# An odd count of expert items: pairs in the loop and a single item behind it

## The chip, the cores and the metric

The kernel runs on one core of a Trainium2 chip. The metric is the device time of one execution in microseconds (us). Before the change three executions took 1818.12, 1817.78 and 1817.76 us, a median of 1817.78.

## The reference

The reference is one layer of a decoder: an HGRN2 recurrence and a gated short convolution side by side, an output projection with a residual, then a mixture of experts, and a last RMS norm. The change touches the routed experts alone:

```python
T = 1024 tokens (16 meta tokens ahead of them are dropped at the end), D_MODEL = 1024
N_EXPERTS, TOP_K, EXPERT_FF = 64, 8, 256

scores = sigmoid(xt @ w_router)
_, top_idx = top_k(scores + router_bias, TOP_K)
gates = scores[top_idx] / sum(scores[top_idx]) * 2.5
for each expert e, for each token t that chose it:
    routed[t] += gate[t, e] * (silu(x[t] @ w_gate_e[e]) * (x[t] @ w_up_e[e])) @ w_down_e[e]
```

There are 1024 x 8 = 8192 assignments, 128 to an expert in the mean.

## The kernel before

**Items.** The routed work is cut into items. One item is one expert with up to CAP = 160 of its tokens; an expert with more than 160 gets further items. So there are 64 + X items, where X counts the further ones. The table of items has room for ITEMS = 118; unused entries are padding: they name an expert, but their rows lie behind the real ones (rows 1024 and up) and their gates are zero.

An item's tokens are 128 main rows (gathered to `XG`) and up to 32 rest rows. The rest rows of two items (a pair, with q = 0 and q = 1) are gathered together (to `XR`, 64 rows). Per item the kernel turns X by TensorE transposes (L1510, and L1518 for the pair's rest), computes gate and up in float32 (L1530, 64 matmuls), sigmoid and products (ScalarE L1614, VectorE L1670 to L1676), splits the down matrix into a high and a low part (`WH` on ScalarE L1601, `WL` on VectorE L1665), and computes down for the rest rows in float32 (L1541, 16 matmuls) and for the main rows from the parts (L1552 to L1554, 12 matmuls). ScalarE evicts the results with the gate as scale (`YF` L1620, `YE` twice in L1624), and POOL adds them to the accumulator in HBM by two indirect DMAs with an addition, the rest rows from `YF` (L1449) and the main rows from `YE` (L1453).

**How many.** `phase_out_route` writes the count of pairs less one to `K.pairs` (L1291 to L1293): 31 plus the number of the entries of `twos` (0, 2, 4, ... from the iota in L923) that are below X. Each engine reads it as `last`.

**Turns.** Every engine runs `turn_(i, q, ahead)` with n = 2i + q. In a turn, TensorE first computes gate and up of item n + 1 (`ahead` of 1 or more), turns the rows of item n + 2 (`ahead` of 2; for q = 0 the next pair's rest rows too), and then does down of item n (`down_rest`, then `down` twice). The loop runs full turns for i from 0 to last - 1. Behind it, written out, stand the turns of the last pair: `turn_(last, 0, 1)` and `turn_(last, 1, 0)`.

**Queues around it.** SP loads the weights in the loop: in each turn gate and up of item n + 3 (L1408), once TensorE is done with gate and up that lie in that place, and down of item n + 2 (L1409), once VectorE and `down_rest` are done with item n. At its end it waits for the last gate and up (L1412). POOL in each turn copies the gates of item n + 1, waits until TensorE has turned, and gathers item n + 4 (L1422) and for q = 0 the rest rows of pair i + 2 (L1430). Then `add_rows` (L1438) waits until both scatters of item n - 1 have landed (`s_ad`, L1441), copies the indices (L1444), waits for `YF` and issues L1449, waits for `YE` and issues L1453. At the end it waits until all of them have landed (L1499); after that block comes `phase_final`, whose first load of the accumulator is L1718.

Of the kernel before, what the change touches and what calls it, by code (L numbers as in the profile page):

```python
# [775 lines left out]
def phase_out_route(nc, ins, K, xn2_d, acc_d, tbl_d):  # L776
# [4 lines left out]
    with ExitStack() as ctx:  # L781
# [130 lines left out]
        @block.gpsimd  # L912
        def _(pool):
            pool.memset(junk, 0.0).then_inc(s_z, 1)
            pool.iota(fill[:, :, 0], [[1, CAP]], base=T, channel_multiplier=0, allow_small_or_imprecise_dtypes=True).then_inc(s_fi, 1)
            pool.memset(fill[:, :, 1:2], 0.0).then_inc(s_fi, 1)
            pool.memset(before[:, :], 1.0).then_inc(s_k0, 1)
            pool.memset(pairsel[:, :], 1.0).then_inc(s_k0, 1)
            pool.iota(lowi[:, :], [[0, 1]], base=0, channel_multiplier=1, allow_small_or_imprecise_dtypes=True).then_inc(s_k0, 1)
            pool.iota(rowc[:, :], [[0, 1]], base=0, channel_multiplier=CHUNKS, allow_small_or_imprecise_dtypes=True).then_inc(s_k0, 1)  # L920
            pool.iota(e0[:, :], [[CHUNKS * CAP, E_N]], base=1, channel_multiplier=0, allow_small_or_imprecise_dtypes=True).then_inc(s_k, 1)
            pool.iota(pidx[:, :], [[0, 1]], base=-E_N, channel_multiplier=1, allow_small_or_imprecise_dtypes=True).then_inc(s_k, 1)
            pool.iota(twos, [[2, 32]], base=0, channel_multiplier=0, allow_small_or_imprecise_dtypes=True).then_inc(s_k, 1)  # L923
            pool.iota(pay[:, :, :, 0], [[P, TT], [0, TOPK]], base=0, channel_multiplier=1,
                      allow_small_or_imprecise_dtypes=True).then_inc(s_k, 1)
            pool.wait_ge(s_k0, 4)

            pool.affine_select(out=before[:, :], in_=before[:, :], compare_op=ALU.is_gt, fill=0.0,
                               base=0, pattern=[[1, P]], channel_multiplier=-1).then_inc(s_k, 1)
            pool.affine_select(out=pairsel[:, :], in_=pairsel[:, :], compare_op=ALU.is_ge, fill=0.0,  # L930
                               base=0, pattern=[[-2, PAIRS]], channel_multiplier=1).then_inc(s_k0, 1)
            pool.wait_ge(s_k0, 5)
            pool.affine_select(out=pairsel[:, :], in_=pairsel[:, :], compare_op=ALU.is_ge, fill=0.0,
                               base=1, pattern=[[2, PAIRS]], channel_multiplier=-1).then_inc(s_k, 1)

            pool.wait_ge(s_fo, 16 * -(-TABLE_ROWS // P))
            for j in range(TT):
                pool.wait_ge(s_pay, j + 1)
                for k in range(TOPK):
                    pool.indirect_dma_start(tbl_d, bass.IndirectOffsetOnAxis(ap=si[:, j * TOPK + k:j * TOPK + k + 1], axis=0),  # L940
                                            pay[:, j, k, :], None).then_inc(s_sca, 16)
            pool.wait_ge(s_row, 1)
            pool.wait_ge(s_sca, 16 * TT * TOPK)
            pool.indirect_dma_start(tbl.rearrange("i c w -> i (c w)"), None, tbl_rows,
                                    bass.IndirectOffsetOnAxis(ap=rowi[:, :], axis=0)).then_inc(s_ti, 16)
            pool.wait_ge(s_ag, 16 * len(SLOT_TILES))
            pool.memset(K.slot[2][2 * CAP1:, :], 0.0).then_inc(s_xr, 1)
            pool.wait_ge(s_ix, 1)
            pool.indirect_dma_start(K.slot[0], None, xn2_d, bass.IndirectOffsetOnAxis(ap=K.idx[0][:, 0:1], axis=0)) \
                .then_inc(K.s_g[0], 16)  # L950
            pool.wait_ge(s_xr, 1)
            pool.indirect_dma_start(K.slot[2][0:2 * CAP1, :], None, xn2_d, bass.IndirectOffsetOnAxis(ap=K.rest[:, 0:1], axis=0)) \
                .then_inc(K.s_gr, 16)
            pool.indirect_dma_start(K.slot[1], None, xn2_d, bass.IndirectOffsetOnAxis(ap=K.idx[0][:, 1:2], axis=0)) \
                .then_inc(K.s_g[1], 16)
            pool.wait_ge(s_ti, 16)
# [373 lines left out]
def phase_experts(nc, ins, K, xn2_d, acc_d):  # L1330
# [3 lines left out]
    with ExitStack() as ctx:  # L1334
# [46 lines left out]
        @block.sync  # L1381
        def _(sp):
            def load(n, q, matrices):

                e = sp.value_load(K.expert[0:1, bass.ds(n, 1)], min_val=0, max_val=E_N - 1)
                for k in matrices:
                    src = weights[k]
                    if k == 2 and not isinstance(n, int):
                        sp.wait_ge(s_dlo, n - 1)
                        sp.sem_inc(turn["sp"], 1)  # L1390
                        sp.wait_ge(s_yr, n - 1)
                        sp.sem_inc(turn["sp"], 1)
                    elif k == 0:
                        sp.wait_ge(s_gu, n * 2 - 2)
                        sp.sem_inc(turn["sp"], 1)
                    sp.dma_start(WR[q][k][:, :].rearrange("p (o t f) -> p o t f", o=1, t=src.shape[2]), src[:, bass.ds(e, 1), :, :]) \
                        .then_inc(s_raw[q][k], 16)

            for q in two:
                for k in two:  # L1400
                    sp.sem_inc(s_raw[q][k], 16)
            sp.sem_inc(s_raw[0][2], 16)
            load(1, 1, (2,))
            load(2, 0, (0, 1))
            last = pairs(sp)
            with sp.Fori(0, last) as i:
                for q in two:
                    load(i * 2 + (q + 3), 1 - q, (0, 1))  # L1408
                    load(i * 2 + (q + 2), q, (2,))  # L1409

            for k in two:
                sp.wait_ge(s_raw[0][k], last * 16 + 32)  # L1412
                sp.sem_inc(turn["sp"], 1)

        @block.gpsimd
        def _(pool):
# [72 lines left out]
                for q in two:  # L1489
                    turn_(i, q, 2)  # L1490
            for q in two:
                turn_(last, q, 1 - q)

            for q in two:
                pool.wait_ge(s_g[q], last * 16 + 32)
                pool.sem_inc(turn["pool"], 1)
            pool.wait_ge(s_gr, last * 16 + 32)
            pool.sem_inc(turn["pool"], 1)
            pool.wait_ge(s_ad, last * 64 + 64)  # L1499
            pool.sem_inc(turn["pool"], 1)  # L1500

        @block.tensor
        def _(pe):
# [83 lines left out]
            with pe.Fori(0, last) as i:  # L1587
                for q in two:
                    turn_(i, q, 2)
            for q in two:  # L1590
                turn_(last, q, 1 - q)

        @block.scalar
        def _(act):
# [31 lines left out]
            def turn_(i, q, ahead):  # L1626
                n = i * 2 + q
                high_down(q, n, i + 1)
                if ahead >= 1:
                    sigmoid(0, n + 1)  # L1630
                if ahead >= 2:
                    keep(0, q, n + 2)
                    keep(1, q, n + 2)
                if ahead >= 1:
                    sigmoid(1, n + 1)
                if ahead >= 2 and q == 0:
                    keep_rest(0, i + 1)
                    keep_rest(1, i + 1)
                evict_rest(q, n)
                for g in two:  # L1640
                    evict(q, n, g)
# [10 lines left out]
            with act.Fori(0, last) as i:  # L1652
                for q in two:
                    turn_(i, q, 2)
            for q in two:
                turn_(last, q, 1 - q)

        @block.vector
        def _(dve):
            step = Chain(dve, s_hc)  # L1660
            tt = nc.vector.tensor_tensor

            def low_down(q, n):
                dve.wait_ge(s_dhi, n + 1)
                tt(WL[q][:, :], WR[q][2][:, :], WH[q][:, :].bitcast(F32), ALU.subtract).then_inc(s_dlo, 1)  # L1665

            def hidden(f, q, n):

                dve.wait_ge(s_ss, n * 2 + f + 1)
                step(tt(SS[:, f, :], SS[:, f, :], gu[f][:, 0, :], ALU.mult))  # L1670
                if f == 0:
                    dve.wait_ge(s_y, n * 2 + 1)
                step(tt(HF[q][:, f, :], SS[:, f, :], gu[f][:, 1, :], ALU.mult))
                dve.sem_inc(s_gk, 1)
                step(nc.vector.tensor_copy(HH[q][:, f, :], HF[q][:, f, 0:P]))
                tt(HL[q][:, f, :], HF[q][:, f, 0:P], HH[q][:, f, :].bitcast(F32), ALU.subtract).then_inc(s_he, 1)  # L1676

            def turn_(i, q, ahead):
                n, o = i * 2 + q, 1 - q
                low_down(q, n)  # L1680
                if ahead >= 1:
                    hidden(0, o, n + 1)
                    hidden(1, o, n + 1)

            hidden(0, 0, 0)
            hidden(1, 0, 0)
            last = pairs(dve)
            with dve.Fori(0, last) as i:
                step.enter(i, 12)
                for q in two:  # L1690
                    turn_(i, q, 2)
            step.leave(last)
            for q in two:
                turn_(last, q, 1 - q)


def phase_final(nc, ins, K, acc_d, out):
# [89 lines left out]
```

## Time and profile before

| what | before |
|---|---|
| median of three executions | 1817.78 us |
| the profiled execution, its time | 1817.95 us |
| its span, first to last instruction | 1816.2 us |
| mean granted TensorE clock | 0.965 of full speed |
| the stage of the experts | about 841 to 1791 us of the span |
| the final norm behind it | 1791 to 1816 us |

The profile is of one execution. The span leaves out what lies around the first and the last instruction, so it is 1.75 us shorter than that execution's time. The engines are PE (TensorE's matmuls), PEld (its weight loads, which overlap them), DVE (VectorE), ACT (ScalarE), POOL (GpSimd) and SPq (the DMA issues of SyncE). A row of the timeline gives start and duration in us, engine, line, operation, and in brackets how long the engine sat idle ahead of it and what ended that.

### The profile page before, as it was taken

Reading aid. Unit: us, or ns where it says so; the run is one execution under the profiler, and the core shown is the slowest. Engines: PE = TensorE matmul, PEld = TensorE weight load, DVE = VectorE, ACT = ScalarE, POOL = GpSimd, SP = SyncE. Lnnn points to the kernel's source line nnn. Section 1 sums busy time; section 2 is a strip of 40 time slices with the busy share of each in tenths; the row PEclk is TensorE's granted clock in tenths of the full one; section 3 lists DMA queues with packets and bytes.
Section 4 is the critical chain, followed back from the end, with each engine's and each line's share of the span. In section 5 each row is a group of like instructions: output and inputs, shape, how many; then the busy total and the mean of one; then the engine's idle time right before and its main releaser. Section 6 shows DMA issues by size and latency. Waiting matters only on the chain. (4 is left out here: it accounts for less than half of the span.)

```text
span 1816.2 us, 29882 instructions
## 1 busy us (share of the span) xinstructions
PE 1686.2 (93%) x10076; PEld 1336.2 (74%) x10076; DVE 737.5 (41%) x1532; ACT 632.8 (35%) x1004; POOL 644.0 (35%) x790
## 2 busy tenths in 40 slices
PE   4989899999998899997999999999999999999981
PEld 3767655655554356675999999999999999999970
DVE  5010266666665676541333333333333333333332
ACT  7111233333333332111434433444344334443433
POOL 1200000025552122331544554445455444554540
PEclk9989899999999899998999999999999999999995
DMA  4011100010006101143999999999999999999986
GB/s 141 1 47 35 35 24 23 23 34 24 23 12 250 65 24 48 47 163 131 305 319 322 318 322 312 323 325 313 318 316 317 327 310 323 328 310 320 321 259 222
DMA packets 111949, 348.68 MB, mean 192 GB/s; under 512 B 14591, under 2 KB 48064, under 8 KB 94510
## 3 DMA queue, kind: packets, MB, share of 16 engines
q1 hardware_dynamic: 78094, 260.23, 39.7%
q0 software_dynamic: 33824, 88.06, 20.0%
q8 instruction: 16, 0.26, 0.1%
q14 instruction: 15, 0.12, 0.0%
HBM read 290.46 MB, written 57.79 MB: 192 GB/s over the span
## 5 line engine op out<-in xcount | busy, mean ns | idle before, releaser
L1530 PE MATMUL gu<-XS,place 128*128 128x160 f32 x4224 | 597.1, 300 | 0.7 <-ACT XS L1609 0.7
L1530 PEld LDWEIGHTS gu<-XS,place 128*128 128x128 f32 x4224 | 584.3, 190 | 6.2 <-ACT XS L1609 1.1
L1665 DVE TENSOR_TENSOR WL<-place,WH 128x2048 fp32r<-128x2048 f32 x66 | 152.1, 2305 | 339.0 <-ACT WH L1601 339.0
L469 PE MATMUL bank<-xT,wi 128*128 128x512 f32 x512 | 241.6, 613 | 0.0
L1614 ACT ACTIVATE SS<-gu 128x160 f32<-128x160 f32 x132 | 40.2, 304 | 372.3 <-PE gu L1530 372.3
L469 PEld LDWEIGHTS bank<-xT,wi 128*128 128x128 f32 x512 | 93.5, 194 | 90.4 <-issue 90.4
L1670 DVE TENSOR_TENSOR SS<-SS,gu 128x160 f32<-128x160 f32 x132 | 41.7, 316 | 261.1 <-ACT SS L1614 261.1
L357 POOL TENSOR_TENSOR place<-place 128x514 f32<-128x514 f32 (+1 forms) x8 | 12.0, 1494 | 371.5 <-ACT place L539 371.2
L1435 POOL COPY gta<-tables 128x1 f32 (+1 forms) x66 | 130.4, 1977 | 11.7 <-POOLq L781 11.7
L1624 ACT ACTIVATE YE<-ype,gta 128x512 f32<-128x512 f32 x132 | 91.0, 690 | 112.4 <-PE ype L1554 112.4
L940 POOL DMA_INDIRECT slot_table<-pay,si x64 | 63.2, 988 | 183.7 <-DVEq L1238 166.7
L1449 POOL DMA_INDIRECT acc_rows<-YF,sib x66 | 105.4, 1596 | 61.1 <-POOL sib L1444 56.6
L1601 ACT ACTIVATE WH<-place 128x2048 fp32r<-128x2048 f32 x66 | 125.5, 1902 | 0.7 <-issue 0.7
L1453 POOL DMA_INDIRECT acc_rows<-YE,sia x66 | 112.0, 1697 | 27.5 <-issue 24.5
L1552 PE MATMUL ype<-WH,hidh 128*128 128x512 f32 x264 | 111.4, 422 | 0.0
L1554 PE MATMUL ype<-WH,hidr 128*128 128x512 f32 x264 | 104.2, 395 | 0.0
L1553 PE MATMUL ype<-WL,hidh 128*128 128x512 f32 x264 | 103.8, 393 | 0.0
L1435 POOL COPY gtb<-tables 128x1 f32 (+1 forms) x66 | 92.1, 1396 | 0.0
L1422 POOL DMA_INDIRECT wi<-xn_rows,gi x66 | 67.3, 1020 | 55.1 <-POOL gi L1419 55.1
L458 PEld LDWEIGHTS sc<-wi 128*128 128x128 f32 x448 | 57.5, 192 | 34.5 <-issue 34.0
L1605 ACT COPY XS<-xp 128x512 f32<-128x512 f32 x132 | 71.0, 589 | 31.1 <-PE xp L1510 22.5
L1552 PEld LDWEIGHTS ype<-WH,hidh 128*128 128x128 f32 x264 | 49.8, 189 | 36.0 <-issue 27.6
(279 smaller groups left out, 2506.0 us busy)
## 6 DMA issues: line engine op xcount, KB each, us to landing
place<-in_w_gate_e SPq DMA_DIRECT2D x67, 1024.0 KB
place<-in_w_up_e SPq DMA_DIRECT2D x67, 1024.0 KB
place<-in_w_down_e SPq DMA_DIRECT2D x66, 1024.0 KB
wi<-in_w_in SPq DMA_DIRECT2D x16, 512.0 KB, 3.9
xn_rows<-place SPq DMA_DIRECT2D x9, 512.0 KB, 2.6
xt<-in_x SPq DMA_DIRECT2D x8, 512.0 KB, 5.7
wbuf<-in_w_in SPq DMA_DIRECT2D x8, 512.0 KB, 4.1
wo<-in_w_out SPq DMA_DIRECT2D x2, 2048.0 KB, 10.2
```

The source lines that it names most:

```text
L469: last = pe.matmul(bank[blk][:, :], wbuf[s][:, t, :], K.xT[:, t, cols], start=(t == 0), stop=(t == KT - 1))
L1435: last = pool.tensor_copy(gt[q][r][:, :], K.gate[r][:, bass.ds(n, 1)])
L1449: pool.indirect_dma_start(acc_q, bass.IndirectOffsetOnAxis(ap=si[q][1][:, :], axis=0), YF[q][:, :], None, compute_op=ALU.add).then_inc(s_a ...
L1453: pool.indirect_dma_start(acc_d, bass.IndirectOffsetOnAxis(ap=si[q][0][:, :], axis=0), YE[q][:, :], None, compute_op=ALU.add).then_inc(s_a ...
L1530: last = pe.matmul(gu[f][:, k, :], raw[:, t, f * P:f * P + P], XS[:, q, t, :], start=(t == 0), stop=(t == KT - 1))
L1552: pe.matmul(yp[g][:, :], hh, high[:, f, cols], start=(f == 0), stop=False)
L1553: pe.matmul(yp[g][:, :], hh, low[:, f, cols], start=False, stop=False)
L1554: last = pe.matmul(yp[g][:, :], hl, high[:, f, cols], start=False, stop=(f == 1))
L1601: act.activation(WH[q][:, :], WR[q][2][:, :], ACT.Copy).then_inc(s_dhi, 1)
L1605: act.copy(XS[:, q, 4 * h:4 * h + 4, 0:P], xp[h][:, :, :]).then_inc(s_xk, 1)
L1624: act.activation(YE[q][:, 512 * g:512 * g + 512], yp[g][:, :], ACT.Copy, scale=gt[q][0][:, 0:1]).then_inc(s_ya, 1)
L1665: tt(WL[q][:, :], WR[q][2][:, :], WH[q][:, :].bitcast(F32), ALU.subtract).then_inc(s_dlo, 1)
```

## The change

The iota starts from 1 in place of 0, so `K.pairs` counts 1, 3, 5, ... below X. TensorE, ScalarE and VectorE get three written-out turns behind the loop: a full one for q = 0, one that looks a single item ahead for q = 1, and one that only finishes item 2 * last + 2. POOL's three turns gather nothing more. SP loads the down matrix of the single item behind the loop (its gate and up come from the loop) and doesn't wait at its end. POOL's last wait counts two more DMAs (32) beside `last`.

```diff
@@ phase_out_route, gpsimd
-            pool.iota(twos, [[2, 32]], base=0, channel_multiplier=0, allow_small_or_imprecise_dtypes=True).then_inc(s_k, 1)
+            pool.iota(twos, [[2, 32]], base=1, channel_multiplier=0, allow_small_or_imprecise_dtypes=True).then_inc(s_k, 1)
@@ phase_experts, sync
-            for k in two:
-                sp.wait_ge(s_raw[0][k], last * 16 + 32)
-                sp.sem_inc(turn["sp"], 1)
+            load(last * 2 + 2, 0, (2,))
@@ phase_experts, gpsimd
             for q in two:
-                turn_(last, q, 1 - q)
+                turn_(last, q, 1)
+            turn_(last + 1, 0, 0)
...
-            pool.wait_ge(s_ad, last * 64 + 64)
+            pool.wait_ge(s_ad, last * 64 + 96)
@@ phase_experts, tensor, and the same in scalar and vector
-            for q in two:
-                turn_(last, q, 1 - q)
+            turn_(last, 0, 2)
+            turn_(last, 1, 1)
+            turn_(last + 1, 0, 0)
```

## Rows read from the trace of the kernel before

**Rows 1.** The page: its span and the first of its engines.
```profile
span 1816.2 us, 29882 instructions
PE 1686.2 (93%) x10076; PEld 1336.2 (74%) x10076; DVE 737.5 (41%) x1532; ACT 632.8 (35%) x1004; POOL 644.0 (35%) x790
```

**Rows 2.** Groups by line, 700 to 1816 us: busy, mean ns, idle before.
```profile
L1530 PE MATMUL gu<-XS,place 128*128 128x160 f32 x4224 | 597.1, 300 | 0.7 <-ACT XS L1609 0.7
```

**Rows 3.** DMA issues of the whole run: count, KB each, us to landing.
```profile
place<-in_w_gate_e SPq DMA_DIRECT2D x67, 1024.0 KB
...
place<-in_w_down_e SPq DMA_DIRECT2D x66, 1024.0 KB
...
wi<-xn_rows,gi POOLq DMA_INDIRECT x66, 7.6
```

**Rows 4.** Stretches: length, busy PE, PEld, DVE, ACT, POOL, clock, DMA, GB/s.
```profile
1500.00:1700.00 200.00, 200.00 (x1487) 182.47 (x1486) 64.23 (x127) 82.28 (x129) 100.68 (x130) 1.00 1.01 321
```

**Rows 5.** PE's waits, 800 to 1816 us: total us, times, longest.
```profile
PE yrest L1541 <- DVE WL L1665: 5.1, 1, 5.1
PE xp L1510 <- PEq L781: 4.6, 1, 4.6
```

**Rows 6.** Timeline, the first down_rest matmul of a turn (for 882.32 its weight load).
```profile
882.32 0.59 PEld L1541 LDWEIGHTS yrest<-place,HF 128*32 128x32 f32 x16 [0.17 <-issue]
...
1720.71 1.07 PE L1541 MATMUL yrest<-place,HF 128*32 128x256 f32 x16
...
1735.12 1.07 PE L1541 MATMUL yrest<-place,HF 128*32 128x256 f32 x16
...
1748.66 1.07 PE L1541 MATMUL yrest<-place,HF 128*32 128x256 f32 x16
...
1761.31 1.07 PE L1541 MATMUL yrest<-place,HF 128*32 128x256 f32 x16
...
1770.41 1.94 PE L1541 MATMUL yrest<-place,HF 128*32 128x256 f32 x16 [5.09 <-DVE WL L1665]
```

**Rows 7.** SP: two loads of the timeline, and one of SP's waits.
```profile
1734.54 0.34 SPq L1396 DMA_DIRECT2D place<-in_w_gate_e  x1
...
1736.48 0.39 SPq L1396 DMA_DIRECT2D place<-in_w_down_e  x1
...
SPq L1413 <- DMA place<-in_w_gate_e: 5.1, 1, 5.1
```

**Rows 8.** Timeline, the last turns: evictions, WL, POOL's scatters, first load behind.
```profile
1724.77 0.69 ACT L1624 ACTIVATE YE<-ype,gta 128x512 f32<-128x512 f32 x1 [0.67 <-PE ype L1554]
...
1726.24 1.56 POOL L1453 DMA_INDIRECT acc_rows<-YE,sia  x1 [0.84 <-ACT YE L1624]
...
1740.70 1.57 POOL L1453 DMA_INDIRECT acc_rows<-YE,sia  x1 [0.40 <-issue]
...
1741.72 2.31 DVE L1665 TENSOR_TENSOR WL<-place,WH 128x2048 fp32r<-128x2048 f32 x1 [5.65 <-ACT WH L1601]
...
1751.63 0.18 POOL L1444 COPY sia<-tables 128x1 int32 x1 [4.96 <-DMA acc_rows<-YE,sia]
...
1765.36 0.69 ACT L1624 ACTIVATE YE<-ype,gta 128x512 f32<-128x512 f32 x1 [0.67 <-PE ype L1554]
...
1767.88 2.29 DVE L1665 TENSOR_TENSOR WL<-place,WH 128x2048 fp32r<-128x2048 f32 x1 [4.74 <-ACT WH L1601]
1768.33 3.26 POOL L1453 DMA_INDIRECT acc_rows<-YE,sia  x1 [0.30 <-issue]
...
1776.22 0.19 POOL L1444 COPY sia<-tables 128x1 int32 x1 [4.63 <-DMA acc_rows<-YE,sia]
...
1776.89 0.69 ACT L1624 ACTIVATE YE<-ype,gta 128x512 f32<-128x512 f32 x1 [0.95 <-PE ype L1554]
...
1779.34 1.54 POOL L1453 DMA_INDIRECT acc_rows<-YE,sia  x1 [0.30 <-issue]
...
1791.05 0.33 SPq L1718 DMA_DIRECT2D A<-acc_rows  x1
```

More of the change, by code:

```diff
@@ L1654, in _ @@
                     turn_(i, q, 2)
-            for q in two:
-                turn_(last, q, 1 - q)
+            turn_(last, 0, 2)
+            turn_(last, 1, 1)
+            turn_(last + 1, 0, 0)
         @block.vector
@@ L1692, in _ @@
             step.leave(last)
-            for q in two:
-                turn_(last, q, 1 - q)
+            turn_(last, 0, 2)
+            turn_(last, 1, 1)
+            turn_(last + 1, 0, 0)
 def phase_final(nc, ins, K, acc_d, out):
```

## The prediction

> **What bounds the kernel now.** I read the page first, for the span and the engines [rows 1]: TensorE is busy for 93% of 1816.2 us. Then I read the groups of the routed experts' stage and its DMA issues [rows 2, 3]. There are 4224 gate and up matmuls, 64 to an item, so 66 items are computed; 67 gate matrices, as many up matrices and 66 down matrices are loaded, and 66 main gathers start inside the stage (the first two are issued ahead of it). So the queue fetches more than the items need. Next comes the question which of TensorE and DMA sets the pace, since the stretch table has both full: TensorE 200.00 of 200.00 us, DMA share 1.01, 321 GB/s, clock 1.00 [rows 4]. TensorE's list of waits settles it: in the whole stage it waited 4.6 us for its own sequencer at the start and 5.1 us for WL at the end, and never for a transfer [rows 5]. Its timeline says the same by turns. I take the first `down_rest` matmul of each item as a mark (turn n computes gate and up of item n+1 and down of item n). From 1720.71 to 1735.12 is 14.41 us, a turn with q=0, which also turns the rest rows; from there to 1748.66 is 13.54 us, a turn with q=1 [rows 6]. These two numbers alternate over the whole stage: from the mark at 882.32 to that at 1748.66 are 31 pairs of turns in 866.34 us, 27.95 a pair, which is 14.41 + 13.54. A stage paced by a memory queue would not repeat so exactly. The last two turns are shorter, 12.64 and 9.10 us, since they have less ahead to compute.
>
> **How many items there must be.** The table gives 64 + X items, where X counts experts' further chunks of 160 tokens. The reference's router on its own inputs, less the 16 meta tokens, gives the largest loads as 165, 160, 155 and 154 of 8192 assignments: X = 1. (66 items in the trace fit X = 1 or 2.) Before, the pair count is 31 + ceil(X/2) = 32, with two more turns behind the loop. After, iota base 1 makes it 31 + floor(X/2) = 31, with three turns behind the loop: 65 items, and item 65, which was all padding, is gone.
>
> **The parts, costed.**
> - *TensorE.* Before: 32 pairs of full turns, then the turn with gate and up only, then down alone. After: 31 pairs, one full q=0 turn written out, then the same two short ones. The difference is exactly one full q=1 turn: 13.54 us [rows 6], all of it on the path, as TensorE has no idle time there.
> - *Code.* The q=0 turn now runs outside the loop. No row shows that turn there, so I bound it. Above stands TensorE's 4.6 us wait for its sequencer at the stage's start [rows 5]; below stands 0, as the short turn behind the loop began without idle time (12.64 us, a q=1 turn without its transposes). A gain is excluded, since full turns in the loop already have no gap. I take 0, the nearer row, being the same loop's exit. ScalarE and VectorE have idle time in each turn. The iota's new base costs nothing: same instruction, and not near the end of anything.
> - *SP's queue.* Loads of 5 matrices fall away: gate, up and down of item 65, gate and up of item 66. Item 64's down load is issued at the same place in its turn as before, behind `down_rest` of item 62 (near 1736.5, the place of the row at 1736.48 [rows 7]), and is needed one turn later, near 1752.4; it now has no 2 MB of gate and up from 1734.54 ahead of it. SP's closing wait for item 66's gate and up goes (the gate's alone was 5.1 us [rows 7]), on a queue that then had nothing to do until 1791. Worth 0.
> - *POOL's queue.* Two gathers and a rest gather (items 66 and 67) go, with their index copies. POOL waits in each turn for the landing of the previous item's scatters, so here it matters what follows the PE work. I work it out in the clock of before.
>  PE, ScalarE and VectorE do turns up to 62 as before, so item 62's YE scatter starts at 1740.70 or up to 0.5 earlier [rows 8]. In before it landed so that POOL moved on at 1751.63, 10.9 us later, in a full DMA. With the weights gone I take 7.9 us, the time from 1768.33 to 1776.22, where DMA was nearly idle: 1748.6. Then YF of item 63 and, 0.8 us behind the eviction, YE follow (the lag: an eviction ending at 1725.46 and a scatter at 1726.24 [rows 8]). Item 63's last eviction ends at 1766.05 - 13.54 = 1752.5, so YE is issued at 1753.3, in place of 1768.33 - 13.54 = 1754.8. It thus starts ahead of WL (1767.88 - 13.54 = 1754.34). In before it started behind WL's start and took 3.26 us in place of 1.54. It ends at 1754.9 and lands 4.6 us later (1771.59 to 1776.22), at 1759.5. The last item's YE then no longer waits for POOL's chain but for its own eviction, which ends at 1776.89 + 0.69 - 13.54 = 1764.04: issue at 1764.84, against 1779.34 - 13.54 = 1765.80. Gain: **0.96 us**. Bounds: 0, if the landing stays at 10.9 us, and about 2, if the last scatter also lands sooner because YF's rows, issued 1.9 us ahead of it, are out of its way. I take 0.96, since DMA in that stretch will be like the near-idle one.
> - *The end.* From the last YE issue to the first load of the final norm is 11.71 us (1779.34 to 1791.05), and 25.2 us behind it. Unchanged.
>
> The 3.26 us row is a long scatter issue that starts inside WL. A page of the Trainium skill has a rule on this (SBUF — State Buffer, SBUF: two separate sides): VectorE and GpSimd share a port pair under an exclusive lock, and descriptors aren't written while VectorE holds it. Read strictly, item 63's YE would end only behind WL, near 1757.2, land near 1761.8, and let the last YE go at 1764.96; the sum would be 14.4 in place of 14.5. The row at 1740.70 (1.57 us, though WL ran from 1741.72) speaks against the strict reading.
>
> **Sum:** 13.54 + 0.96 = 14.5 us. The profiled execution is 1817.95 us (span 1816.2 and 1.75 around it), so 1803.45 and a span of 1801.7. The median of three runs lies 0.17 below it: **1803.3 us**.
>
> **The rivals.**
> 1. *The tail keeps its chain.* Only the turn goes and POOL's waits shift whole: 1817.78 - 13.54 = 1804.2. For it: the last three turns' order on every queue is the same. Against it: DMA load there falls. 18%.
> 2. *A stall behind the loop.* The unrolled turn waits for code on TensorE by the 4.6 us of [rows 5]: 1803.3 + 4.6 = 1807.9. Against it: no gap at the loop's exit now. 6%. The Trainium skill (Runtime: NRT & Kernel Launch, Instruction fetch mechanics) says that a taken branch breaks sequential fetch and straight code does not; by that rule nothing is added here, as in my sum.
> 3. *DMA is the pace.* Then what counts is bytes: 5 matrices of 1.05 MB, two gathers of 0.52, a rest gather of 0.26 and scatters of 0.66, together 7.2 MB, at 321 GB/s [rows 4] 22.4 us: 1795.4. For it: a DMA share of 1.01. Against it: the waits and the exact turns. 3%.
> 4. *Slower: X is even.* If the router on the chip gives the expert with 160 tokens one more, X = 2; before it is 66 items all the same, but the changed kernel then does 67, a padded one at the end. The price is one q=0 turn: 1817.78 + 14.41 = 1832.2, less up to 1 in the tail. It decides at one token. For it: 160 is on the edge, and the trace cannot tell 65 from 66 real items. Against it: it needs a near tie to fall otherwise than in the reference. 2%.
>
> **How the numbers follow.** My forecast has 70%, with 1 for what I have not named, near no change. The range is the forecast's bounds and the first rival with some spread of the runs (0.36 us before): 1801.8, from a tail gain of 2 and 0.5 for spread, to 1804.9, from no tail gain and 0.7 for spread. A measurement of this kernel can tell about 0.2%, 3.6 us, from no change. Faster by more: 0.97 (the forecast and rivals 1, 2 and 3). Slower: 0.02 (rival 4). The same: 0.01.
>
> **What would show it.** The page should have 65 WL subtractions, 4160 gate and up matmuls, 65 loads of each matrix, 64 main gathers and 32 rest gathers in the stage. The marks should run 14.41, 12.64, 9.10 at the end, the last near 1756.86. The penultimate YE issue should take about 1.55 us and not 3.26, and the last come near 1764.8 with its wait ended by ScalarE's eviction. The final norm's first load should start near 1776.5. I am wrong if there are 67 items, if a gap stands between the loop and the next turn, or if turns in the loop are not 14.41 and 13.54.

## The result and the profile after

| what | before | after |
|---|---|---|
| median, range of the executions | 1817.77 us (1817.58 to 1818.12, four) | 1803.24 us (1801.18 to 1805.14, four) |
| ratio after to before, 95% interval | | 0.9913 (0.9898 to 0.9928) |
| the profiled execution | 1817.95 us | 1801.69 us |
| its span | 1816.2 us | 1799.9 us |

The change takes 14.5 us off the medians. The forecast was 1803.3. That the two agree to 0.1 us is partly luck: the four executions after it spread over 4 us, and the two profiled ones lie 16.3 us apart. In two later sets of executions (below) both kernels ran some 5 us faster, and the changed kernel's median lay 14.2 and 13.6 us below that of before. So I read the result from the traces, stage by stage.

The page of the changed kernel, its span and engines [rows 1], a group [rows 2], and its DMA issues [rows 3]:

```profile
span 1799.9 us, 29556 instructions
PE 1671.2 (93%) x9976; PEld 1323.4 (74%) x9976; DVE 734.7 (41%) x1523; ACT 627.0 (35%) x996; POOL 636.3 (35%) x778
...
L1529 PE MATMUL gu<-XS,place 128*128 128x160 f32 x4160 | 587.4, 299 | 0.7 <-ACT XS L1609 0.7
...
L1420 POOL DMA_INDIRECT wi<-xn_rows,gi x64 | 65.0, 1015 | 53.4 <-POOL gi L1417 53.4
...
place<-in_w_gate_e SPq DMA_DIRECT2D x65, 1024.0 KB
```

4160 gate and up matmuls are 65 items; a gate matrix is loaded once for each, in place of 67 times for 66. X is 1, as worked out from the reference's router: 66 items before allow X = 1 or 2, and with X = 2 the changed kernel would compute 67.

The stretch table of the changed kernel, same columns as [rows 4], and TensorE's waits [rows 5], from 700 us on:

```profile
1500.00:1700.00 200.00, 200.00 (x1491) 182.68 (x1490) 65.24 (x127) 81.67 (x128) 101.57 (x129) 1.00 1.01 322
```

```profile
PE yrest L1540 <- DVE WL L1666: 5.1, 1, 5.1
PE xp L1509 <- PEq L781: 4.6, 1, 4.6
```

The steady part is the same, and no new wait stands among the written-out turns. Its timeline, the first `down_rest` matmul of the last turns [rows 6], and the first mark of the stage:

```profile
867.66 1.07 PE L1540 MATMUL yrest<-place,HF 128*32 128x256 f32 x16
...
1719.60 1.07 PE L1540 MATMUL yrest<-place,HF 128*32 128x256 f32 x16
...
1734.01 1.07 PE L1540 MATMUL yrest<-place,HF 128*32 128x256 f32 x16
...
1746.67 1.07 PE L1540 MATMUL yrest<-place,HF 128*32 128x256 f32 x16
...
1755.77 1.94 PE L1540 MATMUL yrest<-place,HF 128*32 128x256 f32 x16 [5.08 <-DVE WL L1666]
```

The marks of the last items are 14.41, 12.66 and 9.10 us apart: the full q=0 turn, now outside the loop, takes what it took inside. The tail on POOL, ScalarE and VectorE [rows 8]:

```profile
1739.71 1.54 POOL L1451 DMA_INDIRECT acc_rows<-YE,sia  x1 [0.30 <-issue]
...
1746.20 0.18 POOL L1442 COPY sia<-tables 128x1 int32 x1 [3.15 <-DMA acc_rows<-YE,sia]
...
1752.19 1.54 POOL L1451 DMA_INDIRECT acc_rows<-YE,sia  x1 [1.47 <-ACT YE L1624]
1753.24 2.29 DVE L1666 TENSOR_TENSOR WL<-place,WH 128x2048 fp32r<-128x2048 f32 x1 [4.74 <-ACT WH L1601]
...
1758.68 0.18 POOL L1442 COPY sia<-tables 128x1 int32 x1 [4.95 <-DMA acc_rows<-YE,sia]
...
1760.75 1.57 POOL L1447 DMA_INDIRECT acc_rows<-YF,sib  x1 [1.76 <-issue]
1761.91 0.69 ACT L1624 ACTIVATE YE<-ype,gta 128x512 f32<-128x512 f32 x1 [0.70 <-PE ype L1553]
1763.38 1.54 POOL L1451 DMA_INDIRECT acc_rows<-YE,sia  x1 [1.06 <-ACT YE L1624]
...
1774.94 0.34 SPq L1720 DMA_DIRECT2D A<-acc_rows  x1
```

The last but one YE scatter is issued ahead of WL and takes 1.54 us, where it took 3.26 behind WL's start; it lands earlier, and the last one waits for its own eviction ("ACT YE") and no longer for POOL's chain ("issue").

**Where the 16.3 us between the two traces went.** I cut each trace at three instants: the first mark of the stage (868.78 before, 867.66 after), the last mark, and the last YE issue; the final norm's first load is the fourth.

| stretch | before | after | difference |
|---|---|---|---|
| start to the first mark | 868.78 | 867.66 | 1.12 |
| first mark to last mark | 901.63 | 888.11 | 13.52 |
| last mark to last YE issue | 8.93 | 7.61 | 1.32 |
| last YE issue to the final norm's first load | 11.71 | 11.56 | 0.15 |
| behind that | 25.15 | 24.96 | 0.19 |

The first row is no work of the change, since that code is the same but for the iota's base; the first mark stands at 867.66, 864.59 and 863.61 in the three traces of the changed kernel. The number that carries the rest is **first mark to the final norm's first load: 922.27 us before, 907.28 after, 14.99 less**. I compare the experiments by it. The kernel before was traced once, so 922.27 is one execution's number; three traces of the changed kernel give 907.28, 907.14 and 907.19.

### The profile page after: what moved, and what is told of

Same layout as the page of the kernel before. It is cut to its first block and busy times, and to the rows that moved or that the text cites. A ratio compares the mean times of both kernels' runs of the same rounds, so it can differ in the third digit from the quotient of the medians.

```text
span 1799.9 us, 29556 instructions
## 1 busy us (share of the span) xinstructions
PE 1671.2 (93%) x9976; PEld 1323.4 (74%) x9976; DVE 734.7 (41%) x1523; ACT 627.0 (35%) x996; POOL 636.3 (35%) x778
## 5 line engine op out<-in xcount | busy, mean ns | idle before, releaser
L1529 PE MATMUL gu<-XS,place 128*128 128x160 f32 x4160 | 587.4, 299 | 0.7 <-ACT XS L1609 0.7
L1529 PEld LDWEIGHTS gu<-XS,place 128*128 128x128 f32 x4160 | 574.9, 190 | 6.0 <-ACT XS L1609 1.1
L357 POOL TENSOR_TENSOR place<-place 128x514 f32<-128x514 f32 (+1 forms) x8 | 11.4, 1422 | 369.9 <-ACT place L539 369.6
L1433 POOL COPY gta<-tables 128x1 f32 (+1 forms) x65 | 126.0, 1938 | 10.5 <-POOLq L781 10.5
L1451 POOL DMA_INDIRECT acc_rows<-YE,sia x65 | 116.5, 1792 | 30.0 <-issue 24.7
L1433 POOL COPY gtb<-tables 128x1 f32 (+1 forms) x65 | 83.5, 1285 | 0.0
L1540 PE MATMUL yrest<-place,HF 128*32 128x256 f32 x1040 | 70.5, 389 | 5.1 <-DVE WL L1666 5.1
```

The lines of the kernel that those rows point to most:

```text
L1433: last = pool.tensor_copy(gt[q][r][:, :], K.gate[r][:, bass.ds(n, 1)])
L1451: pool.indirect_dma_start(acc_d, bass.IndirectOffsetOnAxis(ap=si[q][0][:, :], axis=0), YE[q][:, :], None, compute_op=ALU.add).then_inc(s_a ...
L1529: last = pe.matmul(gu[f][:, k, :], raw[:, t, f * P:f * P + P], XS[:, q, t, :], start=(t == 0), stop=(t == KT - 1))
L1540: last = pe.matmul(yr[j * CAP1:(j + 1) * CAP1, :], HF[q][:, f, P:CAP], raw[:, f, j * DQ:(j + 1) * DQ], start=(f == 0), stop=(f == 1), tile ...
```

## The experiments

The experiments ran in three sets. In two of them the kernel before itself spread over 1808.37 to 1815.18 us (15 executions, median 1812.12) and 1808.28 to 1817.46 us (11, median 1812.36); in the third, of a single execution of each kernel, it took 1818.01. So their medians tell a microsecond from another poorly, and their traces tell it well. "Stage" below is first mark to the final norm's first load.

**The changed kernel again.**

> The changed kernel unchanged, to see its spread. Its four times fell in two pairs, 1801.2 and 1801.7, 1804.8 and 1805.1, where before spreads over 0.5 us. Theory A (the turn and the tail come off exactly; the spread comes from the stages ahead of the experts, where the granted clock rises at other moments): in the trace the marks from the first full turn on stay 14.41 and 13.54 apart and the tail as seen, and a time that differs does so ahead of 880 us. Theory B (the tail behind the loop is what varies, as its DMA order is new): the marks before 1700 us agree to 0.5 us and the difference stands behind them. Median 1801 to 1805 by both.

Measured: 1797.93 us (1795.05 to 1798.57, five), ratio 0.9915 (0.9902 to 0.9929), so 14.2 us less than before again. Stage 907.14 us, 0.14 from the first trace, though its first mark stands at 864.59 and not at 867.66. Theory A holds, with one correction: the clock makes its difference in the tail too (below). The gain is the same on a base that moves.

**The useless transfers put back.** The excerpt leaves out POOL's waits at its end and the bound of the item table.

```diff
+            load(last * 2 + 3, 1, (0, 1))
             load(last * 2 + 2, 0, (2,))
+            for k in two:
+                sp.wait_ge(s_raw[1][k], last * 16 + 32)
+                sp.sem_inc(turn["sp"], 1)
@@ gpsimd
-            for q in two:
-                turn_(last, q, 1)
+            turn_(last, 0, 2)
+            turn_(last, 1, 1)
...
```

> The changed kernel with useless transfers put back in the last full turn: gate and up of item 65 (2 MB) ahead of item 64's down matrix, waited for by SP at the end, and the gathers of item 66 and its rest rows. 65 items as in the change. Theory A (a part of the gain is the DMA load that falls away in the tail, so that POOL's chain of scatters no longer sets the end): slower than the changed kernel by 1.0 to 1.5 us, about 1804.2, with the last but one YE scatter issued inside WL and 3.26 us long again. Rival (the tail shifts as a whole and these transfers cost nothing): within 0.3 us of the changed kernel, its scatters where they were.

Measured: 1800.11 us (1799.04 to 1804.22, five), 0.9934 (0.9920 to 0.9947). Stage 908.72 us, 1.44 and 1.58 above the two traces of the changed kernel, and 13.55 below before: one q=1 turn, 13.54. That the two agree to 0.01 us is luck in part, as the last YE issue comes 9.11 us behind the last mark (8.93 before) and the final norm's first load 11.50 us behind that (11.71 before). Its timeline:

```profile
1747.00 0.19 POOL L1446 COPY sia<-tables 128x1 int32 x1 [7.63 <-DMA acc_rows<-YE,sia]
...
1749.56 2.29 DVE L1670 TENSOR_TENSOR WL<-place,WH 128x2048 fp32r<-128x2048 f32 x1 [4.75 <-ACT WH L1605]
...
1750.07 3.20 POOL L1455 DMA_INDIRECT acc_rows<-YE,sia  x1 [0.30 <-issue]
...
1758.08 0.18 POOL L1446 COPY sia<-tables 128x1 int32 x1 [4.82 <-DMA acc_rows<-YE,sia]
...
1759.33 1.57 POOL L1451 DMA_INDIRECT acc_rows<-YF,sib  x1 [0.94 <-POOL sib L1446]
1761.20 1.54 POOL L1455 DMA_INDIRECT acc_rows<-YE,sia  x1 [0.30 <-issue]
```

The scatter before lands late (7.63 us of waiting in place of 3.15), the next is issued inside WL and takes 3.20 us, and the last is set by POOL's chain. That is before's tail, on a kernel with 65 items. The slow link is the third YE scatter from the end: from its issue to POOL's next index copy are 11.10 us here (1735.90 to 1747.00), and 6.49 in the changed kernel (1739.71 to 1746.20). The other traces agree: 8.9 to 11.1 us in the four where the transfers run on (10.12 before), 6.4 to 6.8 us in the eight where they are gone and such a copy follows the landing. So the fallen transfers shorten the chain, and the rival, that the tail shifts whole, is out. This run puts weights and gathers back together and doesn't tell which of them delays the scatter.

How much of that reaches the end is another question. The last eviction ends 7.53 us behind the last mark here and 6.83 in the changed kernel, as the granted clock rose later (6.0 against 4.5 us behind the mark). A last YE issue 0.78 us behind its eviction, as in the changed kernel, would have come at 8.31 and not 9.11: POOL's chain costs 0.8 us here, and by the same reckoning 1.0 before (8.93 for 7.17 + 0.78). The other 0.7 is the clock's. The kernel with 64 items (below) has the useless transfers too, and its chain came through in time:

```profile
1739.31 1.54 POOL L1453 DMA_INDIRECT acc_rows<-YE,sia  x1 [0.57 <-issue]
...
1740.37 2.29 DVE L1665 TENSOR_TENSOR WL<-place,WH 128x2048 fp32r<-128x2048 f32 x1 [4.75 <-ACT WH L1601]
...
1751.09 1.54 POOL L1453 DMA_INDIRECT acc_rows<-YE,sia  x1 [2.45 <-ACT YE L1624]
```

There the slow scatter took 9.25 us, the next one was issued ahead of WL, and the last one waited for its eviction, which ended 7.41 us behind the mark. So the useless transfers cost 0.8 and 1.0 us at the end of two traces and nothing in that one.

**Only the useless transfers taken away, 66 items.** The excerpt leaves out the bounds of the pair count and POOL's last wait, which counts two more items.

```diff
-            step(ts(K.pairs[:, :], pr, float(E_N // 2 - 1), None, ALU.add))
+            step(ts(K.pairs[:, :], pr, float(E_N // 2 - 2), None, ALU.add))
@@ behind the loop of tensor, scalar and vector
             for q in two:
-                turn_(last, q, 1 - q)
+                turn_(last, q, 2)
+            for q in two:
+                turn_(last + 1, q, 1 - q)
@@ behind the loop of gpsimd
             for q in two:
-                turn_(last, q, 1 - q)
+                turn_(last, q, 1)
+            for q in two:
+                turn_(last + 1, q, 1 - q)
@@ sync
+            load(last * 2 + 3, 1, (0, 1))
+            load(last * 2 + 2, 0, (2,))
+            load(last * 2 + 3, 1, (2,))
...
```

> The kernel before with its 66 items, but the last full pair written out behind the loop, so that nothing is loaded or gathered for items 66 and 67. Theory A: 1.0 to 1.5 us faster than before, about 1816.5, from the tail alone, with all turns 14.41 and 13.54 apart and the last mark at the same place as before (1770.4 less what the start of the stage gives). Rival 1 (nothing in the tail depends on it): within 0.3 us of before. Rival 2 (written-out turns wait for code): slower than before, by up to 4.6 us at the loop's exit. Rival 3 (DMA is the pace): faster by 2 matrices and two and a half gathers, 3.4 MB or 10 us.

Measured: 1811.37 us (1807.97 to 1814.56, eleven), 0.9997 (0.9988 to 1.0007), so the times show no difference. Stage 921.67 us, only 0.60 below before, where I expected 1.0 to 1.5. Its marks still alternate and end with 13.54, 12.64, 9.11, so a loop left one pair earlier costs nothing, and rival 3, DMA as the pace (10 us), is out. POOL's part came as expected: the last index copy stands 2.90 us behind the last mark (1766.24 to 1763.34) and not 5.81 (1776.22 to 1770.41). The rest was given back at the last eviction:

```profile
1763.34 1.94 PE L1543 MATMUL yrest<-place,HF 128*32 128x256 f32 x16 [5.09 <-DVE WL L1671]
...
1770.32 0.69 ACT L1628 ACTIVATE YE<-ype,gta 128x512 f32<-128x512 f32 x1 [1.46 <-PE ype L1556]
...
1771.78 1.54 POOL L1453 DMA_INDIRECT acc_rows<-YE,sia  x1 [2.72 <-ACT YE L1628]
```

TensorE idles 5.1 us ahead of the last down, and the granted clock is at 0.50, half of 2.4 GHz, when it starts again. When it rises differs from execution to execution: 4.5 us behind the last mark in the changed kernel's trace, 5.2 before, 6.3 here. The last eviction ended 6.83, 7.17 and 7.67 us behind the mark, in the same order. Since now the eviction sets the end, the 0.5 us between here and before counts; without it the gain would be 1.0 to 1.1.

**67 items, the parity falling the other way.**

```diff
-            step(ts(K.pairs[:, :], pr, float(E_N // 2 - 1), None, ALU.add))
+            step(ts(K.pairs[:, :], pr, float(E_N // 2), None, ALU.add))
```

> The changed kernel with a pair count higher by one, so that it computes 67 items, the last two all padding: the price of the parity falling the other way. Theory A: the changed kernel plus one pair of turns, 14.41 + 13.54 = 27.95 us, about 1831.2, and 14.4 less up to 1.3 in the tail above before, so 13.0 to 13.5 slower than before. Rival (padded items cost less or more than real ones, since their gathers and scatters go to neighbouring rows): the turns of items 65 and 66 would stand out from 14.41 and 13.54.

Measured: 1823.67 us (1822.86 to 1825.98, four), 1.0065 (1.0050 to 1.0080) of before, 11.6 us above its median. Stage 935.89 us: 13.62 above before (13.0 to 13.5 expected; the clock rose 5.4 us behind the last mark, and the last eviction ended 7.23 behind it), and 28.6 above the changed kernel (27.95). The turns that compute gate and up of the padded items 65 and 66 take 14.41 and 12.66 us (marks from 1739.91 to 1754.32 and 1766.98), as the same turns do with real ones. So rival 4's price was right by the traces (the medians give less, 11.6): with an even count this change costs nearly what it gains with an odd one. It is a stand-in: no run had a router that gives X = 2.

**64 items.**

```diff
-            pool.iota(twos, [[2, 32]], base=0, channel_multiplier=0, allow_small_or_imprecise_dtypes=True).then_inc(s_k, 1)
+            pool.iota(twos, [[2, 32]], base=1, channel_multiplier=0, allow_small_or_imprecise_dtypes=True).then_inc(s_k, 1)
```

> The kernel before with the iota's base at 1 alone, so it does 64 items and leaves out the item of the fullest expert's last 5 tokens. Together with the others it gives a ladder of 64, 65, 66 and 67 items. Theory A: from the first mark of the stage to the final norm's first load 27.95 us less than before's 922.27, so 894.3, and the changed kernel's 907.1 to 907.3 lies a q=0 turn above it less the tail's 1.3 to 1.5, so 13.0 above. Rival (the last items, as padding, are cheaper): not on this ladder.

Measured: 1792.56 us in its single execution; stage 895.97 us, 1.65 above the 894.3 expected, so the changed kernel stands only 11.3 above it and not 13.0. The marks are right (the last at 1742.90, 873.68 behind the first; before's 901.63 less 27.95 is 873.68). The last YE issue comes 0.74 sooner behind its mark than before (8.19, as above). From there to the final norm's first load it takes 14.10 us, where 11.4 to 11.8 is what all the others take. The DMA engines move nothing more from 1757 on, 8 us ahead of that load, so it is no slow transfer. I have no explanation for these 2.4 us.

**Which engine is the pace.** Two kernels, the changed one with fewer bytes and the changed one with fewer matmuls, each executed once (1795.36 and 1739.07 us):

> The changed kernel with only half of each up matrix loaded in the stage (0.52 MB less of about 4.5 MB in every turn; the other half of the place keeps what an earlier item left, so the result is not the reference's). Theory A (TensorE is the pace): marks 14.41 and 13.54 apart as before, the span within its spread, only POOL's waits for landed scatters shorter. Rival (DMA is the pace): each turn 12% shorter, 1.6 us, and 100 us off the whole.

> The changed kernel without the matmuls that multiply the low part of the down matrix (L1552 of the changed kernel, 4 of 0.23 us in a turn; the result loses that part's precision). Theory A: turns of 13.49 and 12.62 us, 60 us off the whole, as long as DMA follows: the same bytes in a turn shorter by 0.92 us are 343 GB/s in place of 321. Rival (DMA is just as full as TensorE): turns stay near 14.41 and 13.54, and TensorE's list shows waits for the gate and up loads.

```profile
1300.00:1500.00 200.00, 200.00 (x1492) 182.64 (x1492) 66.83 (x131) 81.11 (x130) 102.67 (x130) 1.00 0.96 282
```

```profile
1300.00:1500.00 200.00, 200.00 (x1533) 183.87 (x1532) 71.14 (x140) 86.63 (x139) 102.69 (x141) 1.00 1.03 341
...
PE yrest L1540 <- DVE WL L1665: 5.1, 1, 5.1
```

The first row is the kernel with half of each up matrix: 282 GB/s in place of 322, and turns of 14.41 and 13.54 still (stage 907.12 us). The second is the kernel without the low product, with its only wait of TensorE from 860 us on: turns of 13.51 and 12.63, 58.6 us off the stage (848.68), and DMA simply moved 341 GB/s at a share of 1.03. So a DMA share of 1.01 didn't mean that DMA was full. TensorE is the pace, by removal and not only by its list of waits.

**The long scatter issue.**

```diff
@@ vector, the very last turn of the kernel before
-                low_down(q, n)
+                low_down(q, n, ahead == 0)
@@ vector, low_down
                 dve.wait_ge(s_dhi, n + 1)
+                if skip:
+                    dve.sem_inc(s_dlo, 1)
+                    return
```

> The kernel before without VectorE's computation of the low part in the very last turn (it signals at once; the last item's low part is that of an earlier one, so its result is not the reference's; that item is padding). Theory A (a scatter issue that starts inside this instruction is held up by it): the last but one YE scatter's issue is 1.55 us long in place of 3.26, though nothing of POOL is changed, and the last mark comes 2.3 us sooner behind its neighbour, at 6.8 in place of 9.10. Rival (the long issue comes from something else, such as descriptors waiting for room): it stays at 3.2 us.

```profile
1763.51 1.54 POOL L1453 DMA_INDIRECT acc_rows<-YE,sia  x1 [0.30 <-issue]
```

Measured: 1812.34 us in its single execution. The issue takes 1.54 us in place of 3.26, and the last mark stands 6.84 us behind its neighbour. But this run alone doesn't show the cause. POOL saw the scatter ahead land sooner than before (8.94 us behind its issue, and not 10.12), so this issue started at 1763.51, while WH was still being made:

```profile
1762.31 1.90 ACT L1601 ACTIVATE WH<-place 128x2048 fp32r<-128x2048 f32 x1
```

WL couldn't have started before 1764.21, so with WL in place the issue would have been ahead of it all the same. What ties the long issues to WL is the timing over all thirteen traces. 94 of the 1698 scatter issues of the stage take longer than 1.65 us (2.04 to 3.67). Each of them starts inside WL, 0.06 us or more behind its start, and each ends 1.42 to 1.44 us behind WL's end, wherever inside it started. All the others take 1.54 to 1.65 us; among them are the only five that started inside WL by less, at most 0.04 us. One of the 94, from the loop of the kernel with the transfers put back (ends at 1724.78 and 1726.22):

```profile
1722.49 2.29 DVE L1670 TENSOR_TENSOR WL<-place,WH 128x2048 fp32r<-128x2048 f32 x1 [4.75 <-ACT WH L1605]
...
1722.79 3.43 POOL L1455 DMA_INDIRECT acc_rows<-YE,sia  x1 [0.30 <-issue]
```

So a long issue is one that waits for WL to end. The Trainium skill (SBUF — State Buffer, SBUF: two separate sides) says that VectorE and GpSimd share a port pair under an exclusive lock, which whichever starts first keeps for its whole instruction. The timing agrees with that for a scatter that starts inside WL; that it is a port, no run shows. For a scatter that starts first the traces show no delay, be it by 1 us ([rows 8] at 1740.70) or by 0.08, as these rows of the changed kernel show:

```profile
1726.10 1.56 POOL L1451 DMA_INDIRECT acc_rows<-YE,sia  x1 [0.30 <-issue]
1726.18 2.29 DVE L1666 TENSOR_TENSOR WL<-place,WH 128x2048 fp32r<-128x2048 f32 x1 [4.75 <-ACT WH L1601]
```

That fits the page too. The strict reading in the prediction, by which such a scatter would end only behind WL, is wrong.

**A shorter tail.** The 5.1 us of idle time ahead of the last down come from order alone: WH of the last item stands on ScalarE behind the evictions, though its weights landed long before. In the last turn but one both engines have idle time:

```diff
@@ scalar, turn_
-                high_down(q, n, i + 1)
                 if ahead >= 1:
+                    high_down(q, n, i + 1)
                     sigmoid(0, n + 1)
+                if ahead == 1:
+                    high_down(1 - q, n + 1, i + 2)
@@ vector, turn_
-                low_down(q, n)
                 if ahead >= 1:
+                    low_down(q, n)
                     hidden(0, o, n + 1)
+                    if ahead == 1:
+                        low_down(o, n + 1)
                     hidden(1, o, n + 1)
```

> The changed kernel once more, beside the two versions below and on their chip. From the first mark to the final norm's first load 907.1 to 907.5 us, as in its other two traces.

> The changed kernel with the last item's split of the down matrix (WH and WL) done one turn earlier, in ScalarE's and VectorE's idle time of the last turn but one. Theory A (TensorE's 5.1 us wait ahead of the last down is only in-order ScalarE work behind the evictions, but behind it POOL's chain of landed scatters sets the end): the wait is gone and the last mark comes 4 us behind its neighbour in place of 9.10, but the last YE scatter can go only 1.25 + 1.87 us behind the landing of the one before: 1761.8 in place of 1763.4 on the changed kernel's scale, 1.6 us off the whole. Rival (the end follows TensorE): 5 to 6 us off.

> The same, and POOL copies the scatter's indices ahead of its wait for the landing in place of behind it. Theory A: 1.2 us more, 2.8 us below the changed kernel from the first mark to the final norm's first load, 904.4; turns in the loop unchanged. Rival: POOL's copies now run inside WL in the loop and delay something there, so that the turns grow.

In the last version `add_rows` copies the indices and waits for the copies first, and only then waits for the landing.

| kernel | median (range), six each | ratio to before | stage |
|---|---|---|---|
| changed | 1798.72 us (1798.03 to 1802.70) | 0.9930 (0.9915 to 0.9946) | 907.19 us |
| WH and WL earlier | 1797.45 us (1795.28 to 1800.34) | 0.9916 (0.9901 to 0.9930) | 906.25 us |
| and indices copied ahead | 1795.92 us (1794.95 to 1802.25) | 0.9915 (0.9898 to 0.9933) | 905.93 us |

With WH and WL earlier the timeline reads:

```profile
1746.45 1.07 PE L1540 MATMUL yrest<-place,HF 128*32 128x256 f32 x16
...
1750.40 1.07 PE L1540 MATMUL yrest<-place,HF 128*32 128x256 f32 x16
...
1758.25 0.18 POOL L1442 COPY sia<-tables 128x1 int32 x1 [4.74 <-DMA acc_rows<-YE,sia]
...
1760.32 1.57 POOL L1447 DMA_INDIRECT acc_rows<-YF,sib  x1 [1.76 <-issue]
1762.19 1.54 POOL L1451 DMA_INDIRECT acc_rows<-YE,sia  x1 [0.30 <-issue]
```

TensorE's last wait is gone (the marks are 3.95 us apart and not 9.10), the clock never falls there (1.07 us and not 1.94 for the same group), and yet only 0.9 us of 5.1 arrive at the end: POOL may not scatter the last item before the one ahead has landed, and that is now the last thing waited for (the copy at 1758.25 ends a wait of 4.74 us for the landing). The rival that the end follows TensorE is out. Both versions gained less than I expected (0.9 for 1.6, 1.3 for 2.8). The YF issue came 2.07 us behind the landing's copy in place of the 1.25 that the kernel with the transfers put back shows (1758.08 to 1759.33), with 1.76 us put down to "issue", and that already in the changed kernel (1758.68 to 1760.75). It was not there with 64, 66 and 67 items or with the transfers put back. The kernel with 67 items runs the same instructions on POOL and shows 0.94 us, so the written-out code alone isn't the cause; what it is stays open. The intervals of the three ratios overlap; the gain of these two versions is shown by their traces alone.

## Why the prediction was right

- **The turn taken off.** 13.54 forecast, 13.52 in the two traces (and 13.55 by the stages of before and of the kernel with the transfers put back, where the tail is alike). This step carried nine tenths of the number, and it came from reading which turn falls away: q=1 and not q=0 or their mean, since the full turn written out behind the loop is a q=0 one.
- **The count.** 65 items, X = 1. The price of the other parity was forecast as 14.41 less up to 1, and measured as 13.62 by the stages and 11.6 by the medians.
- **Code behind the loop, SP's queue, the iota: nothing.** The marks behind the loop are 14.41 and 12.66 apart, with no gap.
- **POOL's chain.** 0.96 forecast, 1.32 measured from mark to issue. On the clock of before (1770.41 - 13.54 - 1755.77 = 1.10 us is added to the times of after) the steps were: item 62's landing seen at 1748.6 forecast, 1747.3 measured; YE of item 63 at 1753.3 and 1753.29; landing 1759.5 and 1759.78; the last YE at 1764.84 and 1764.48. The chain is the one described. Item 62's landing was put too late by 1.3 us: the 7.9 us taken for it held an issue of 3.26 us that had waited for WL, and a plain one gives 1.54 + 4.63 = 6.17 by the same rows, where the trace shows 6.49. It did no harm, as item 63's YE waited for its eviction and not for that landing. The 0.36 us that it gained beyond the forecast is the last eviction ending 6.83 us behind the mark and not 7.17, because the granted clock rose 4.5 us behind the mark and not 5.2. I had carried before's eviction over as if the clock's moment were fixed.
- **The tail keeps its chain** had 18%. The medians don't tell it from the forecast: they differ by 14.5, 14.2 and 13.6 us, and it said 13.5. The traces do, by the order in the tail and by 7.61 to 7.65 us from the last mark to the last YE issue in three traces, where before's one trace has 8.93. The kernel with 64 items gave 8.19 with the useless transfers in place, so the 1.32 us are the difference of these traces and not a constant.
- **DMA as the pace** had 3%. Both removals speak against it.
- **The spread.** I took the spread of runs as 0.36 us from three executions. It is several microseconds for either kernel on a wider sample, so the range of 1801.8 to 1804.9 held the median but not all single executions (1801.18 to 1805.14). Later medians of the changed kernel were 1797.93 and 1798.72 us, below the whole range, because before's moved down with them: the difference was forecast soundly, and that the absolute time fitted to 0.1 us is luck. The step that was weak is this one: three close times were taken for the kernel's spread.

## What to carry to other kernels

Where a loop does two things in turn, price the one that the edit really removes; the period's alternation tells it to 0.01 us. A prefetch that runs past the last item is not free even when nobody waits for it: here a scatter beside it took 8.9 to 11.1 us to land in place of about 6.5, which cost 0.8 and 1.0 us of the end in two traces and nothing in a third. And a count rounded to the other parity only moves the cost to inputs of the other kind, so state for which inputs it gains.

## What the runs showed of the hardware that I had not expected

- A DMA busy share of 1.01 at 321 GB/s was no limit: with shorter turns the same loads went at 341 GB/s and 1.03, and TensorE never waited for one of them.
- After 5.1 us without work TensorE came back at half its clock in each of the ten traces that have this wait, and the instant at which it rose again differed by 1.8 us between them (4.5 to 6.3 us behind the last mark). After 2.8 us without work, in the kernel without the last WL, it came back at full clock. At the start of the stage the same shows: the first 32 gate and up matmuls, which begin at half clock, take 6.61 us in before's trace, 6.00 after, 7.62 in the kernel with 66 lean items.
- An indirect DMA's issue that began inside VectorE's subtraction of two float32 tiles (2.29 us), 0.06 us or more behind its start, ended 1.42 to 1.44 us behind the subtraction's end, 94 times of 94, and so took up to 3.67 us in place of 1.54. One that began as little as 0.08 us ahead of it kept 1.54 to 1.57.
